# A depthwise convolution of 31 taps: from diagonal matmuls and VectorE to four taps stacked in narrow weights, with rows shifted through DRAM

## The reference

```python
for i in range(DEPTH):
    h = x + 0.5 * swiglu(rms_norm_2(x, norm_ffn1[i]), w_ffn1_in[i], w_ffn1_out[i])
    u = rms_norm_2(h, norm_mix[i])
    q, k, v, c, g = jnp.split(u @ w_in[i], splits, axis=-1)
    ...
    y_attn = window_attention(q, k, v, sink[i], rel_bias) @ w_attn_out[i]
    c_val, c_gate = jnp.split(c, 2, axis=-1)
    c = c_val * jax.nn.sigmoid(c_gate)
    c = depthwise_conv(c, conv_w[i], conv_b[i])          # 31 taps, 512 features, 15 zeros on either side
    c = jax.nn.silu(layer_norm_2(c, conv_ln_g[i], conv_ln_b[i]))
    y_conv = c @ w_conv_out[i]
    g_attn, g_conv = jnp.split(jax.nn.sigmoid(g), 2, axis=-1)
    h = h + (g_attn * y_attn + g_conv * y_conv) @ w_o[i]
    ...
```

## Time and profile before

| | |
|---|---|
| median of 3 runs | 2140.91 us (2140.39 to 2141.5) |
| the profiled execution | 2141.09 us, of which the span is 2139.3 |
| busy of the span | TensorE 2114.3 us, weight loads 1928.5, VectorE 1686.6, ScalarE 1264.5, GpSimd 13.1 |
| traffic | 415.11 MB, 194 GB/s on average |

### The profile page before, as it was taken

The page is one execution under the profiler, slowest core; times in us unless marked ns, Lnnn a source line. Parts: engine busy times, 40 slices in busy tenths (PEclk is TensorE's granted clock), DMA queues, the critical chain, the costliest instruction groups (busy, mean ns, idle before and its releaser), DMA issues.

```text
span 2139.3 us, 38823 instructions
## 1 busy us (share of the span) xinstructions
PE 2114.3 (99%) x16064; PEld 1928.5 (90%) x16064; DVE 1686.6 (79%) x2649; ACT 1264.5 (59%) x2114; POOL 13.1 (1%) x20
## 2 busy tenths in 40 slices
PE   8999999999999999999999999999999999999999
PEld 6898999999998899998888999888898889998888
DVE  7899689887877688877886777887688767878875
ACT  4765556555855755555655567665476545766554
POOL 0000000000000000000000000000000000000000
PEclk9999999999999999999999999999999999999999
DMA  9565567777644466655555533555555553345553
GB/s 370 194 223 202 180 209 257 245 243 277 211 158 168 159 223 231 198 183 189 186 192 187 171 116 132 205 193 190 187 179 192 191 187 130 124 164 206 191 191 129
DMA packets 116370, 415.11 MB, mean 194 GB/s; under 512 B 13105, under 2 KB 16561, under 8 KB 115682
## 3 DMA queue, kind: packets, MB, share of 16 engines
q1 hardware_dynamic: 116194, 412.63, 56.5%
HBM read 409.42 MB, written 3.16 MB: 193 GB/s over the span
## 4 chain that ended last, share of the span: by engine, by line
PE 90%; ACT 4%; DVE 3%; DMA 2%; issue 1%; POOL 0%; SPq 0%; ACTq 0%; DVEq 0%
PE bank L205 89%; ACT arena L257 3%; DMA raw<-W 1%; DVE arena L212 1%; ACT hi L257 1%; PE bank L209 1%; DVE lo L212 1%; DVE ada L229 0%; ACT L249 0%; ACT L257 0%; DVE arena L220 0%; DMA xT<-x 0%; POOL arena L212 0%; DVE ysl L212 0%; DVE xT L220 0%
## 5 line engine op out<-in xcount | busy, mean ns | idle before, releaser
L205 PE MATMUL bank<-h,hi 128*128 128x256 f32 (+1 forms) x5216 | 1178.1, 312 | 0.0
L257 ACT ACTIVATE hi<-raw 128x1024 fp32r<-128x1024 f32 x656 | 689.0, 1057 | 555.4 <-PE bank L205 499.0
L205 PE MATMUL bank<-h,lo 128*128 128x256 f32 x3312 | 949.8, 287 | 0.1
L205 PEld LDWEIGHTS bank<-h,hi 128*128 128x128 f32 x5216 | 856.1, 190 | 61.8 <-issue 2.6
L212 DVE TENSOR_TENSOR lo<-raw,hi 128x1024 fp32r<-128x1024 f32 x656 | 792.4, 1220 | 86.3 <-ACT hi L257 85.5
L205 PEld LDWEIGHTS bank<-h,lo 128*128 128x128 f32 x3312 | 630.4, 190 | 11.0 <-issue 7.0
L205 PE MATMUL bank<-act,hi 128*128 128x512 f32 x1056 | 370.0, 393 | 0.0
L205 PE MATMUL bank<-act,lo 128*128 128x256 f32 x1056 | 294.7, 279 | 0.0
L205 PEld LDWEIGHTS bank<-act,hi 128*128 128x128 f32 x1056 | 197.9, 187 | 47.3
L205 PEld LDWEIGHTS bank<-act,lo 128*128 128x128 f32 x1056 | 197.9, 187 | 0.0
L257 ACT ACTIVATE arena<-arena 128x256 f32<-128x256 f32 (+4 forms) x202 | 98.6, 493 | 158.5 <-DVE arena L212 151.1
(11 more groups left out here) (156 smaller groups left out, 2007.9 us busy)
## 6 DMA issues: line engine op xcount, KB each, us to landing
raw<-W SPq DMA_DIRECT2D x664, 512.0 KB, 3.3
ada<-WA SPq DMA_DIRECT2D x80, 512.0 KB, 3.7
arena<-WA SPq DMA_DIRECT2D x16, 512.0 KB, 14.3
p_projected<-arena SPq DMA_DIRECT2D x2, 1024.0 KB, 7.4
arena<-scr SPq DMA_DIRECT2D x16, 128.0 KB, 4.7
arena<-p_projected SPq DMA_DIRECT2D x2, 1024.0 KB, 4.7
xT<-x SPq DMA_DIRECT2D x2, 512.0 KB, 5.0
arena<-lora SPq DMA_DIRECT2D x2, 512.0 KB, 9.8
```

The costliest lines, as they stand in the source:

```text
L205: return self.done(lambda e: e.matmul(out, l, r, start=start, stop=stop, skip_group_check=True))
L257: return self.done(lambda e: e.activation(out, in_, f, scale=scale, **kw))
```

## The change

All 31 taps go to TensorE, as 32 with one of zeros. Weights of 128 rows by 32 columns hold four diagonals of 32 x 32, for taps 4n to 4n+3 of 32 features; eight of them (`CQ`) make all taps. The other operand `Xs` must then have the same 32 features on each quarter of the partitions, moved by 0 to 3 columns: SP writes the rows of `Cb` to DRAM and reads them back four times, each a column further. Two pairs of 128 features are done one after the other: for each, 64 matmuls into four strips of 32 columns. The weights `tapw` come from the host in a load of 2 MB a layer. ScalarE adds the bias when it evicts; VectorE has no tap left.

```diff
-CW, CV = 31, 20
+CW, CQ = 31, 8
+CX = 256 + 4 * (CQ - 1)
...
+    s = ["next"] * 5 + [("conv sum", 0)] + ["next"] * 4 + [("conv sum", 2), "next", ("conv total",)]
+    return s + ["next"] * (21 - s.count("next")) + [("mean",), "next", ("square",), "next", ("var",), "next", ("norm",), ("silu",), "next", ("split",)]
...
-        s += [("qkv", l, p) for p in range(3)] + [("v2", l), ("qk norm", l), ("attention2", l)]
+        s += [("qkv", l, 0), ("taps", l, 0), ("qkv", l, 1), ("qkv", l, 2), ("v2", l), ("taps", l, 2), ("qk norm", l), ("attention2", l)]
...
-                        pe.wait_ge(a_cv, ("diag", l, m, j))
-                        pe.wait_ge(v_main, ("c", l, m))
-                        pe.mm(t256(ps(("conv", l, pr)), m - pr), d, Cb[:, m, j:j + 256], j == CV, j == CW - 1).then_inc(
-                            pe_cv, ("tap", l, m, j))
...
+                elif what == "taps":
+                    l, pr = q
+                    o = take(CONV, ("conv", l, pr))
+                    pe.wait_ge(d_taps, ("taps", l))
+                    pe.wait_ge(d_shift[pr // 2], ("shifted", l, pr))
+                    for n in range(CQ):
+                        for j in range(2):
+                            for c in range(4):
+                                i = pe.mm(t256(o, j)[32 * c:32 * c + 32, :], tapw[:, 4 * (pr + j) + c, n, :],
+                                          Xs[:, 4 * (pr + j) + c, 4 * n:4 * n + 256], n == 0 and j == 0, n == CQ - 1)
+                    i.then_inc(pe_main, ("conv", l, pr))
...
-                                    v.wait_ge(v_cv, ("tap", l, m, j - 1))
-                                    x = v.stt(o, Cb[:, m, j:j + 256], w(m, j), o, MUL, ADD)
...
-                        a.act(diag[n % 8], C("ident"), ACT.Identity, scale=P("conv_w_2", l, j * 4 + m)).then_inc(
-                            a_cv, ("diag", l, m, j))
+                    if what == "conv sum":
+                        pr = q[0]
+                        a.wait_ge(pe_main, ("conv", l, pr))
+                        for j in range(2):
+                            a.act(t256(cacc, pr + j), t256(ps(("conv", l, pr)), j), ACT.Identity, bias=P("conv_b_2", l, pr + j)).then_inc(
+                                a_cv, *([("conv sum", l, pr)] if j else []), frees=("conv", l, pr) if j else None)
...
+            def conv_rows(l, pr):
+                s.wait_ge(v_main, ("c", l, pr + 1))
+                s.dma(T["rows"][l][pr // 2], Cb[:, pr:pr + 2, :]).then_inc(d_rows[pr // 2], ("rows", l, pr))
+
+            def conv_shifted(l, pr):
+                s.wait_ge(d_rows[pr // 2], ("rows", l, pr))
+                for n in range(4):
+                    s.dma(Xs[32 * n:32 * n + 32, 4 * pr:4 * pr + 8, :], T["shifted"][l][pr // 2][n]).then_inc(
+                        d_shift[pr // 2], ("shifted", l, pr))
...
+                elif what == "c":
+                    f.tiles(16)
+                    if q[1] == 2:
+                        conv_rows(q[0], 0)
+                    elif q[1] == 3:
+                        conv_shifted(q[0], 0)
...
+                    l, p = q
+                    f.tiles(8)
+                    if p == 0:
+                        conv_rows(l, 2)
+                    elif p == 1:
+                        conv_shifted(l, 2)
+                    f.tiles(8 if p < 2 else 0)
...
+                elif what == "mixer2":
+                    l = q[0]
+                    s.wait_ge(pe_main, ("f down 1", l, 7))
+                    s.dma(tapw.rearrange("p g n i -> p (g n i)"), T["taps"][l]).then_inc(d_taps, ("taps", l))
```

More of the change, by code:

```diff
@@ L513, in build @@
         d_x = [signal(f"dma_x{i}", 16) for i in range(2)]
+        d_rows, d_shift = ([signal(f"dma_{n}{i}", 16) for i in range(2)] for n in ("conv_rows", "shifted"))
         d_hank = [signal(f"dma_hank{i}", 16) for i in range(8)]
@@ L516, in build @@
         d_ada = [signal(f"dma_ada{i}", 16) for i in range(RAWA)]
-        d_crow, d_par0, d_par, d_cst0, d_cst1, d_cst, d_lora, d_small, d_b2, d_scr, d_p, d_pp, d_pq, d_out = (
+        d_crow, d_par0, d_par, d_cst0, d_cst1, d_cst, d_lora, d_small, d_b2, d_scr, d_p, d_pp, d_pq, d_taps, d_out = (
             signal(f"dma_{n}", 16) for n in ("c_row", "par0", "par", "cst0", "cst1", "cst", "lora", "small", "bias2", "scr", "p", "p_out",
-                                             "p_back", "out"))
+                                             "p_back", "taps", "out"))
         negw0, halfa0 = sml[:, 32:40], sml[:, 40:48]
@@ L605, in build @@
         Vt2 = un(5, 1)
[L606 removed]
+        Cb = ar[:, 11 * 256:11 * 256 + 4 * 288].rearrange("p (m t) -> p m t", m=4)
         gA, gC = un(73, 8), un(89, 8)
@@ L613, in build @@
         cacc, cyc, cy2 = un(16, 4), un(20, 4), un(24, 4)
-        diag = [un(61, 4)[:, i * 128:(i + 1) * 128] for i in range(8)]
+        Xs = ar[:, 20 * 256:20 * 256 + 16 * CX].rearrange("p (g t) -> p g t", g=16)
+        tapw = ar[:, 73 * 256:73 * 256 + 512 * CQ].rearrange("p (g n i) -> p g n i", g=16, n=CQ)
         pf, pfh, pfl = un(49, 2), alias("pfh", 51, 2), alias("pfl", 57, 2)
@@ L1049, in conv2 @@
             def conv2(l):
-                taps = [0]
                 def step(what, *q):
[L1053 to L1058, removed]
-                        pe.wait_ge(a_cv, ("diag", l, m, j))
-                        pe.wait_ge(v_main, ("c", l, m))
-                        pe.mm(t256(ps(("conv", l, pr)), m - pr), d, Cb[:, m, j:j + 256], j == CV, j == CW - 1).then_inc(
-                            pe_cv, ("tap", l, m, j))
-                    elif what == "mean":
+                    if what == "mean":
                         o = take(CONV, ("cmean", l))
@@ L1669, in conv2 @@
             def conv2(l):
-                def w(m, j):
-                    return P("conv_w_2", l, j * 4 + m)
                 def step(what, *q):
[L1674 to L1682, removed]
-                                    v.wait_ge(v_cv, ("tap", l, m, j - 1))
-                                    x = v.stt(o, Cb[:, m, j:j + 256], w(m, j), o, MUL, ADD)
[L1685 to L1696, removed]
+                    if what == "conv total":
+                        v.wait_ge(a_cv, ("conv sum", l, 2))
+                        v.tt(cy2[:, 0:512], cacc[:, 0:512], cacc[:, 512:1024], ADD).then_inc(v_cv, ("conv half", l))
+                        v.wait_ge(v_cv, ("conv half", l))
+                        v.tt(cy2[:, 0:256], cy2[:, 0:256], cy2[:, 256:512], ADD).then_inc(v_cv, ("conv total", l))
                     elif what == "mean":
@@ L2345, in conv2 @@
                 return step
-            conv_taps = [(m, j) for pr in (0, 2) for m in (pr, pr + 1) for j in range(CV, CW)]
             def merge(name, l, m, h):
@@ L2838, in sync_program @@
                         load_bias(h)
-                elif what in ("gmlp u", "gate", "gate2", "wout", "wo", "qk", "c"):
+                elif what in ("gmlp u", "gate", "gate2", "wout", "wo", "qk"):
                     f.tiles(16)
+                elif what == "c":
[4 more added lines that the diff above has]
+                        conv_shifted(q[0], 0)
                 elif what == "attention1":
@@ L2938, in stream, with tap_weights @@
     return out.reshape(nblk, 128, BT * 128)
+def tap_weights(inputs):
+    w = np.concatenate([np.asarray(inputs["conv_w_2"], np.float32).reshape(L, CW, 512), np.zeros((L, 4 * CQ - CW, 512), np.float32)], axis=1)
+    w = w.reshape(L, CQ, 4, 4, 4, 32)
+    out = np.zeros((L, 4, 32, 4, 4, CQ, 32), np.float32)
+    i = np.arange(32)
+    for n in range(CQ):
+        for shift in range(4):
+            for m in range(4):
+                for c in range(4):
+                    out[:, shift, i, m, c, n, i] = w[:, n, shift, m, c, :]
+    return out.reshape(L, 128, 512 * CQ)
 def modulation(inputs):
@@ L2961, in program @@
              oneh=din("oneh", (32, 512)), relb=din("relb", (32, 8)),
-             vmask=din("vmask", (8, 512)), flip=din("flip", (128, 128)), p=din("p", (L, 128, 512)))
+             vmask=din("vmask", (8, 512)), flip=din("flip", (128, 128)), p=din("p", (L, 128, 512)), taps=din("taps", (L, 128, 512 * CQ)))
     T["out"] = nc.dram_tensor("out", [128, 2048], F32, kind="ExternalOutput").ap()
@@ L2966, in program @@
     T["pp"] = nc.dram_tensor("p_projected", [L, 128, 2048], F32, kind="Internal").ap()
+    rows = nc.dram_tensor("conv_rows", [L, 2, 2, 128, 288], F32, kind="Internal").ap()
+    T["rows"] = [[rows[l, pr].rearrange("m p t -> p m t") for pr in range(2)] for l in range(L)]
+    T["shifted"] = [[[bass.AP(rows.tensor, (2 * l + pr) * 256 * 288 + n, [[288, 32], [32 * 288, 8], [1, CX]])
+                      for n in range(4)] for pr in range(2)] for l in range(L)]
     T["hank"] = [bass.AP(scr.tensor, 128 * (1 - t), [[1, 128], [512, 8], [1, 256]]) for t in range(2)]
@@ L2988 @@
         crow=np.ascontiguousarray(crow), lnb=np.ascontiguousarray(np.repeat(ln[:, None, :], 128, axis=1)), bs=bs,
```

(2 more changed lines are left out.)

11 lines of the change are left out of this document (removed).

## The result

The changed kernel takes 2151.68 us (2150.41 to 2153.09, 4 runs) where the kernel before takes 2140.86: a ratio of 1.005, interval 1.0038 to 1.0062. It is 10.8 us slower; 2136.9 was forecast, and the range ended at 2144.5. The profiled execution took 2153.09, 12.0 above the profiled one of before and 1.4 above its own median, so what its trace adds up to is to be held against 12.0.

What follows compares the result with a forecast made beforehand. TensorE, busy 99% of the span, was taken as the bound: -37.8 (old taps) + 27.6 (new matmuls) + 1.4 (narrow weights) + 1.2 (DRAM) + 3.6 (attention) = -4.0 us from 2140.9, so 2136.9 us, range 2133 to 2144.5.

Steps and rivals of the forecast that it cites:

- Added: the way through DRAM: Before each layer's first tap run, TensorE waits 0.6 us for shifted rows written to and read from DRAM; 1.2 us.
- the cover: TensorE work between issue of the reads and the first tap run: tiny matmuls and 16 tiles, 6.4 us.
- Rival C: Shifted rows land late before the first tap runs: 2143.7 us at 4 us a layer, 2151.7 at 8; chance 0.13.
- Removed taps: 88 diagonal matmuls leave TensorE in both layers' mixers, 0.43 us each: 37.8 us less.
- Added matmuls: 256 matmuls of 128 x 32 on TensorE, four strips at a time, 128 steps of 0.216 us: 27.6 us more.
- Rival A: Strips on TensorE do not run four at a time: slower, 2164.5 us or 2154.3; chance 0.13.
- the visit: TensorE going to narrow weights and back at each tap run: 0.34 us, four times, 1.4 us in all.
- Attention's four waits: Without taps in its blocks, TensorE waits 0.9 us for ScalarE before each half's transposes, four times: 3.6 us.
- rival B: TensorE does not wait ahead of attention's transposes: faster, 2133.3 us; chance 0.19.
- Edits at nothing: VectorE losing its taps, ScalarE's 8 evictions for 88 diagonals and GpSimd's wider clearing change no time.
- rival D: The gain is on VectorE and nothing happens to TensorE; dismissed as impossible, no chance given.

Runs made afterwards that it cites:

- The wider reads: Changed kernel with each of the four reads of shifted rows filling all 128 partitions instead of 32, same bytes and row length: 2141.22 us.
- the later runs: Changed kernel with each layer's first run of taps after the third qkv projection instead of the first, its eviction one block later: 2136.38 us.
- The matmuls ahead of the wait: Changed kernel with seven 128 x 512 matmuls on constants before TensorE's wait for the shifted rows, to keep it from idling: 2148.21 us.

## Why the prediction was wrong

- **The step that failed** is "Added: the way through DRAM". It put the read of 1136 KB at the pace of the weight loads and of wide reads in the earlier trace rows (512 KB more in 1.4 us, some 370 GB/s) and got 6.4 us, as much as the cover, with 0.6 added for the issues and the short rows. The reads write 32 partitions each, and with them the whole stretch moves only 201 GB/s. 11.8 us from the first issue, some 12 in layer 1, make waits of 5.9 and 6.3 us: 12.2 instead of 1.2. The wider reads show the cause (1.0 instead of 5.9 in layer 0; in layer 1, where one of the four issues took over 2 us in both kernels, 3.3 instead of 6.3), the later runs (no wait) that the rest of the sum stands.
- **A term that was not in it**: the half clock after the idle time. 15.12 - 5.92 - 7.18 = 2.0 us in layer 0; layer 1's run, worked out in the same way, cost 15.85 - 6.3 - 7.18 = 2.4. The matmuls ahead of the wait show it apart from the wait.
- Together 11.0 + 4.4 = 15.4 us on a forecast of -4.0: 11.4. The small misses of the other terms (0.8 on the taps, -0.3 on the runs, -0.2 on attention) make it 11.7, against 12.0 in the profiled executions. Rival C was right that the rows land late, but not in its reason: with the same 1024 short rows, but to all partitions, TensorE waits 1.0 us in layer 0 instead of 5.9. That its bound of 8 us a layer gives 2151.7, what was measured, is luck: the 8 was waiting alone, where in fact it is 5.9 + 2.0 and 6.3 + 2.4 with the half clock. 0.13 was too small a chance for a chain of transfers whose price no row had.
- **Removed taps**: right. 37.8 forecast, 37.0 by the spans (36.5 by the medians) with attention's waits out of the way.
- **Added matmuls**: right. Rival A is out: a run is 7.18 us in place, 32 steps of 0.216 and 0.27 for the visit (0.34 forecast, from two halves). The loads take 110 ns each, four to a step of 0.216, and lie under the matmuls. So the Trainium skill's rule that the prediction cites (TensorE: Matmul & The Clock Gate, "The mechanism" of Part 3), by which they would lie bare, is not borne out for four strips either.
- **Attention's four waits**: right in place and size (3.4 for 3.6); rival B is out.
- **Edits at nothing**: right for VectorE's taps in the kernel before (none, by the run with two of them), so rival D is out. It holds only beside TensorE's taps: without these, 18 of VectorE's 20 cost 2119.13 - 2109.84 = 9.3 us.

Not settled: the 1 to 1.5 us that the kernel without any taps took beyond its waits and the price of the taps, and why one issue of layer 1's reads takes over 2 us where the others take 0.5.

## What to carry to other kernels

Price a new transfer by rows with the same shape at its destination, the number of partitions first, and where there is no such row, leave its reader room: moving the first run of each layer by two projections was worth 15.3 us here, and no wait shows that it cost anything. A wait on the bounding engine costs more than its length when the granted clock falls in it, so look at the clock of the stretch behind each long wait. And an engine with slack has it only in the blocks as they are: take work from the bounding engine and its neighbours' queues (here VectorE's taps ahead of attention's maximum) can bind in its place.

## What the runs showed of the hardware

- With reads from DRAM to 32 partitions each, 8 us of this stretch moved 201 GB/s, and with the same bytes in the same rows of 1136 bytes to 128 partitions 295 GB/s, weight loads included, the queues 0.97 and 0.91 busy.
- Four strips of 128 x 32 run side by side in float32 at 0.216 us a step, with a new weight load for each matmul, as 14.2 us for 256 records with a mean of 380 ns show: none of the loads' 110 ns comes on top.
- TensorE was idle from 1222.9 to 1228.86; the granted clock was 0.50 from 1225.92 to 1232.75, and the ten steps of matmuls in it took 0.43 us each instead of 0.216. Behind waits of 4.2 us in the kernel without TensorE's taps it was 0.50 as well, and in the version with 15 taps on VectorE behind one of 1.5 us; with the wider reads it stayed at 1.00 through a wait of 3.3 us.
